# Splitting the 528-token stages at token 256 and giving weights and operands one address difference

## The chip, the core and the metric

The kernel runs on one core of one Trainium2 chip. The metric is the device time of one execution in microseconds (us), here the median of the runs shown; lower is better. One further execution is recorded by the hardware profiler, and all rows below come from that one.

## The reference

The reference runs two transformer-like blocks after one another on a sequence of 512 tokens with 1024 features, in float32. The first block has two layers, one with differential attention and one with chunked attention, each followed by a layer norm and a gated feed-forward of width 2816. The second block puts 16 learned "meta" tokens in front, so that it works on 528 tokens, and runs two layers of this form:

```
for l in range(DEPTH):
    h = h + hybrid_mixer(rmsnorm(h, norm_mix_g[l]), ...)     # gated linear attention, retention, LRU
    h = h + conv_glu_ffn(rmsnorm(h, norm_ffn_g[l]), ...)     # up, causal conv of 3, silu(gate)*val, down
return rmsnorm(h, final_norm_g)[:, N_META:]
```

Nearly all arithmetic is matrix products with weight matrices: 1024 x 3328 and 1024 x 1024 in a mixer, 1024 x 5632 (up) and 2816 x 1024 (down) in a feed-forward.

## The kernel before

**Numbers and tiles.** A float32 matrix product is made of three products in the format float32r. Each operand is split into a high part and a low part (XH and XL for the activations, WH and WL for the weights), and for each slice k of 128 inputs TensorE adds WL\*XH, WH\*XL and WH\*XH into PSUM. The helper `part` (line 756 of the profile, L756) issues these; the weight slice is the stationary operand (128 x 128), and the activations are the moving one. Every matmul loads its weights anew, so a LDWEIGHTS belongs to each of them; it overlaps the matmul before.

**Units.** The weights come in 534 units. A unit is one output tile of 128 columns with 8 slices of 128 inputs (1024 floats in a partition), or half of a 256-column tile, or one product of a down-projection (5 or 6 slices). SyncE's queue loads units from HBM into `raw`; ScalarE rounds them into WH (L1551, `highs`); VectorE subtracts to get WL (L2193, `lows`); WH and WL have three slots each, of W_PITCH = 1088 floats. `weight_places` says where in its slot a unit lies: "plain" puts slice k at 128\*k plus an offset; "turned" puts it at W_STEP\*((k + turn) % 4) + 128\*(k // 4), with W_STEP = 272. In the kernel before no unit is turned; the units that have an offset are those of the attention layers (48 floats) and the first three of b, f0 and f1 (16 floats).

**Stages.** In order: attention a, its output ao, feed-forward f0, attention b, output bo, feed-forward f1 (all 512 tokens), then mixer m0, its output mo0, feed-forward g0, mixer m1, output mo1, feed-forward g1 (528 tokens). Each feed-forward does 24 up tiles, the first down part (28 products, `down`, L1090), 20 up tiles, and the second down part (28 products). The down-projections are written with seven products of half-size operands in place of eight; their operands lie in FH and FL for f0 and f1, in GHH and GHL for g0 and g1: six slots with seven rows each. Sums of weight blocks that these products need are made by DMAs that GpSimd issues (`weight_sums`), and SyncE's queue fetches them.

**Segments.** 512 tokens fill one PSUM bank, so in the 512-token stages a tile has one moving segment of 512 columns. 528 tokens take two banks, and two segments. `tokens`, `two`, `pair_of` and `segments` put the split at token 272; the first segment ends its bank and the second starts the next one. In m0, mo0, g0 and m1 the segments are 272 and 256 columns; from mo1 on only the tokens from 14 are needed, and they are 258 and 256. The order in a tile is: for each k, for each of the three products, first segment, second segment:

```
for i, (wb, xb) in enumerate(((WL, xh), (WH, xl), (WH, xh))):
    for a, x0, x1 in segs:
        ins = nc.tensor.matmul(P[:, a:a + x1 - x0], weight(u, wb, k), xb[:, kx, x0 - c0:x1 - c0], ...)
```

`wide_tokens` (L854) makes the tiles of 256 output columns in the mixers: there the activations are stationary, a slice of 128 tokens that starts at token 16 + 128\*i, and the weights are moving, 256 columns. `hgrn` (L1354, L1356) and `ret_values` (L1448, L1453) multiply blocks of 128 tokens that start at token 16 and cut them at the split with `segments`.

**Memory plan.** What matters below is an operand's start in floats, modulo 64 (256 bytes), in a partition. XH, XL, WH and WL start at 32. The rows of XH and XL are 512 floats apart in the 512-token stages and 528 (16 modulo 64) in the others. GH and GL (what the mixers' outputs are multiplied from) start at 16 with rows of 528. FH and FL start at 16, rows of 256, slots of 1792 (0 modulo 64). GHH starts at 16 and GHL at 48, with rows of 272 and slots of 1904 (48 modulo 64); g1 uses 256 of each row. A weight slice in a plain unit starts at 32 plus the unit's offset, for every k.

## Time and profile before

| what | value |
|---|---|
| median of 3 runs | 2564.49 us (2563.74 to 2565.13) |
| the profiled execution, its own time | 2568.07 us |
| its span, first to last instruction | 2566.3 us |
| TensorE busy | 2520.3 us, 98% of the span |
| weight loads busy | 2296.5 us, 89% |
| VectorE busy | 1622.9 us, 63% |
| ScalarE busy | 1163.3 us, 45% |
| GpSimd busy | 169.4 us, 7% |
| matmul instructions in the record | 19246 |

A matmul's duration in the record runs from its start to the end of its last column, and neighbours overlap. So the pace of a stream is the distance from one start to the next, which a timeline gives over several matmuls and a window gives by its count. The profiled execution is 3.58 us longer than the median of the runs; its span is 1.8 us shorter than its own time.

### The profile page before, as it was taken

Reading aid. Unit: us, or ns where it says so; the run is one execution under the profiler, and the core shown is the slowest. Engines: PE = TensorE matmul, PEld = TensorE weight load, DVE = VectorE, ACT = ScalarE, POOL = GpSimd, SP = SyncE. Lnnn points to the kernel's source line nnn. Section 1 sums busy time; section 2 is a strip of 40 time slices with the busy share of each in tenths; the row PEclk is TensorE's granted clock in tenths of the full one; section 3 lists DMA queues with packets and bytes.
Section 4 is the critical chain, followed back from the end, with each engine's and each line's share of the span. In section 5 each row is a group of like instructions: output and inputs, shape, how many; then the busy total and the mean of one; then the engine's idle time right before and its main releaser. Section 6 shows DMA issues by size and latency. Waiting matters only on the chain.

```text
span 2566.3 us, 44717 instructions
## 1 busy us (share of the span) xinstructions
PE 2520.3 (98%) x19246; PEld 2296.5 (89%) x19246; DVE 1622.9 (63%) x2784; ACT 1163.3 (45%) x1924; POOL 169.4 (7%) x219
## 2 busy tenths in 40 slices
PE   9999999999999999999999999999999999999998
PEld 7777889889877888989899899999999989999998
DVE  5767756457566665546766557666675754766666
ACT  4554533335455443334554435434444534544443
POOL 0000200100000110110000011001000000200100
PEclk9999999999999999999999999999999999999999
DMA  5222955974322593895311249259652122954975
GB/s 192 89 66 70 255 150 162 294 193 147 103 82 65 158 248 97 268 256 164 140 67 51 69 160 259 84 174 287 157 187 93 65 71 97 263 143 141 291 175 163
DMA packets 104311, 397.33 MB, mean 155 GB/s; under 512 B 10416, under 2 KB 12720, under 8 KB 84272
## 3 DMA queue, kind: packets, MB, share of 16 engines
q1 hardware_dynamic: 60400, 249.07, 28.5%
q0 software_dynamic: 42992, 143.82, 23.9%
q8 instruction: 151, 2.47, 0.4%
q10 hardware_dynamic: 720, 1.57, 0.2%
q14 instruction: 48, 0.39, 0.0%
HBM read 383.80 MB, written 133.30 MB: 201 GB/s over the span
## 4 chain that ended last, share of the span: by engine, by line
PE 88%; DVE 6%; ACT 3%; DMA 2%; issue 1%; SPq 0%; POOL 0%; DVEq 0%; ACTq 0%; POOLq 0%
PE P L756 59%; PE P L1090 13%; PE P L854 3%; PE P L877 3%; PE P L763 2%; DVE WL L2193 2%; ACT WH L1551 1%; PE P L889 1%; DMA raw<-in_wts 1%; PE P L1188 1%; PE P L1209 1%; PE P L1302 1%; PE P L903 1%; PE P L935 1%; DVE X L2289 0%
## 5 line engine op out<-in xcount | busy, mean ns | idle before, releaser
L756 PE MATMUL P<-XH,WL 128*128 128x256 f32 (+3 forms) x3080 | 839.9, 322 | 15.1 <-DVE XL L2525 6.9
L756 PE MATMUL P<-XL,WH 128*128 128x256 f32 (+3 forms) x3080 | 817.0, 314 | 0.0
L756 PE MATMUL P<-XH,WH 128*128 128x256 f32 (+3 forms) x3080 | 816.7, 314 | 0.0
L2193 DVE TENSOR_TENSOR WL<-raw,WH 128x1024 fp32r<-128x1024 f32 (+2 forms) x533 | 573.9, 1079 | 317.7 <-ACT WH L1551 316.1
L1551 ACT ACTIVATE WH<-raw 128x1024 fp32r<-128x1024 f32 (+2 forms) x533 | 498.0, 941 | 465.9 <-PE P L756 223.4
L756 PEld LDWEIGHTS P<-XH,WL 128*128 128x128 f32 x3080 | 517.9, 189 | 61.2 <-DVE XL L2525 9.8
L756 PEld LDWEIGHTS P<-XH,WH 128*128 128x128 f32 x3080 | 516.3, 189 | 35.5
L756 PEld LDWEIGHTS P<-XL,WH 128*128 128x128 f32 x3080 | 515.8, 189 | 33.0
L1090 PE MATMUL P<-GHH,WL 128*128 128x272 f32 (+1 forms) x616 | 178.3, 290 | 9.5 <-DVE WL L2193 9.5
L1090 PE MATMUL P<-GHH,WH 128*128 128x272 f32 (+1 forms) x616 | 177.0, 287 | 0.0
L1090 PE MATMUL P<-GHL,WH 128*128 128x272 f32 (+1 forms) x616 | 177.0, 287 | 0.0
L1090 PE MATMUL P<-FH,WL 128*128 128x256 f32 x616 | 171.6, 279 | 1.9 <-DVE WL L2193 1.9
L1090 PE MATMUL P<-FH,WH 128*128 128x256 f32 x616 | 170.4, 277 | 0.0
L1090 PE MATMUL P<-FL,WH 128*128 128x256 f32 x616 | 170.4, 277 | 0.0
L3047 DVE SCALAR_TENSOR_TENSOR tmp<-P,PP,tmp 128x527 f32<-128x527 f32 (+1 forms) x88 | 66.7, 758 | 143.9 <-ACT tmp L2141 143.9
L689 POOL DMA_DIRECT2D sums<-in_quads x96 | 104.7, 1091 | 524.4 <-DMA sums<-in_quads 524.4
L1090 PEld LDWEIGHTS P<-GHH,WL 128*128 128x128 f32 x616 | 118.0, 192 | 10.9 <-DVE WL L2193 10.8
L2141 ACT ACTIVATE tmp<-P,PP 128x528 f32<-128x528 f32 (+1 forms) x88 | 68.7, 781 | 118.6 <-PE P L756 118.6
L1090 PEld LDWEIGHTS P<-FH,WL 128*128 128x128 f32 x616 | 115.6, 188 | 2.9 <-DVE WL L2193 2.7
L1090 PEld LDWEIGHTS P<-GHL,WH 128*128 128x128 f32 x616 | 118.2, 192 | 0.1
L1090 PEld LDWEIGHTS P<-GHH,WH 128*128 128x128 f32 x616 | 118.0, 192 | 0.0
L1090 PEld LDWEIGHTS P<-FH,WH 128*128 128x128 f32 x616 | 115.9, 188 | 0.0
(373 smaller groups left out, 3789.8 us busy)
## 6 DMA issues: line engine op xcount, KB each, us to landing
raw<-in_wts SPq DMA_DIRECT2D x151, 1024.0 KB, 5.0
sums<-in_quads POOLq DMA_DIRECT2D x32, 1152.0 KB, 28.5
sums<-in_quads POOLq DMA_DIRECT2D x32, 960.0 KB, 24.6
sums<-in_quads POOLq DMA_DIRECT2D x16, 1536.0 KB, 19.6
raw<-sums SPq DMA_DIRECT2D x64, 384.0 KB, 3.4
sums<-in_quads POOLq DMA_DIRECT2D x16, 1280.0 KB, 13.6
raw<-sums SPq DMA_DIRECT2D x64, 320.0 KB, 3.1
raw<-in_wts SPq DMA_DIRECT2D x48, 384.0 KB, 3.6
```

Of the source, the lines that this page charges most:

```text
L689: nc.gpsimd.dma_start(sums_dram[st, ph, mp, :, a:b, 0:n], term, accum_op=ALU.add).then_inc(summed[mp], 16)
L756: ins = nc.tensor.matmul(P[:, a:a + x1 - x0], weight(u, wb, k), xb[:, kx, x0 - c0:x1 - c0], start=start and i == 0, stop=stop and i == 2, ...
L763: ins = nc.tensor.matmul(P[:, a:a + x1 - x0], m, src[:, x0 - c0:x1 - c0], start=start, stop=stop)
L854: ins = nc.tensor.matmul(o, xb[:, k, c0:c1], weight(u + k // 4, wb, k % 4, 256), start=n == 0 and k == 0 and i == 0, stop=k == 7 and i == ...
L877: ins = nc.tensor.matmul(o, xb[:, k, c0 - c:c1 - c], weight(u + k // 4, wb, k % 4, 256), start=n == 0 and k == 0 and i == 0, stop=k == 7 a ...
L889: ins = nc.tensor.transpose(P[:, 512 * b + 128 * j:512 * b + 128 * j + 128], src[:, 128 * j:128 * j + 128], ident)
L903: nc.tensor.matmul(P[:, o:o + ke], q[64 * m:64 * m + 64, lane, 128 * i:128 * i + 128], k[64 * m:64 * m + 64, 2 + lane, 0:ke], start=(j == ...
L1090: ins = nc.tensor.matmul(P[:, 512 * b:512 * b + n], weight(u, wb, q), combined(st, xb, j, OPERAND[p]), start=p not in AFTER and q == 0 and ...
L1551: nc.scalar.activation(weight_rows(u, WH), raw_rows(u), ACT.Copy).then_inc(*act.up("whi", u))
L2141: nc.scalar.activation(y[:, a0:], pair_bank(n % 4)[:, a0:], ACT.Identity, bias=par("fcb", 44 * l + c), scale=PP[:, k:k + 1]).then_inc(*act ...
L2193: nc.vector.tensor_tensor(weight_rows(u, WL), raw_rows(u), weight_rows(u, WH).bitcast(F), ALU.subtract).then_inc(*dve.up("wlo", u))
L3047: nc.vector.scalar_tensor_tensor(y[:, a0 + 1:T], p[:, a0:T - 1], w(1), y[:, a0 + 1:T], ALU.mult, ALU.add).then_inc(*dve.up("conv1", l, n))
```

## The change

Nothing is computed differently except for the order of a few sums. Three things move:

1. The split lies at token 256 (MID): segments of 256 and 272 columns in m0, mo0, g0 and m1, and from mo1 on 256 and 258 (tokens 14 to 270 to 528). The PSUM places of a pair of banks move along.
2. The units of the mixers and of the up-projections of g0 and g1 are turned: slices 272 floats apart in four groups. ScalarE and VectorE write them as four rows of 256, and the host packs the blocks in that order. Turn is 0 for the 256-column units and the output tiles, 1 otherwise; mo1 and g1 also get 14 floats more. The products of the down-projections of g0 get an offset of 16 floats times the operand's row, those of g1 none.
3. GHH and GHL have slots of 1920 floats with rows of 272 in g0 and of 256 in g1.

```diff
@@ weight_places
-    place = [("plain", 0)] * len(plan)
+    place = [("plain", 0, 0)] * len(plan)
     def put(stage, n, kind, amount):
-        place[first[stage] + n] = (kind, amount)
+        place[first[stage] + n] = (kind, amount, 14 if stage in ("mo1", "g1") and kind == "turned" else 0)
...
+    for l in range(2):
+        for n in range(first[f"mo{l}"] - first[f"m{l}"]):
+            put(f"m{l}", n, "turned", 0 if plan[first[f"m{l}"] + n][4] == 256 else (1, 1)[l])
+        for n in range(8):
+            put(f"mo{l}", n, "turned", (0, 0)[l])
+        for ph, (m0, m1) in enumerate(UP_TILES):
+            at = first[f"g{l}B"] - 2 * (m1 - m0) - first[f"g{l}"] if ph else 0
+            for n in range(2 * (m1 - m0)):
+                put(f"g{l}", at + n, "turned", (1, 1)[l])
+            for n, (p, mp) in enumerate(products(ph)):
+                put(f"g{l}{'AB'[ph]}", n, "plain", LINE // 4 * ((OPERAND[p] + (-OPERAND[p] if l else 0)) % 4))
@@ segments of tokens
+MID = 256
 def two(p):
-    a = 1024 * p + 240
-    return [(a, 0, 272), (a + 272, 272, T)]
+    return [(1024 * p + 512 - MID, 0, MID), (1024 * p + 512, MID, T)]
 def segments(c0, c1):
-    return [(a, b) for a, b in ((c0, min(c1, 272)), (max(c0, 272), c1)) if a < b]
+    return [(a, b) for a, b in ((c0, min(c1, MID)), (max(c0, MID), c1)) if a < b]
+def mid(s):
+    return MID + META - 2 if s == 6 else MID
 def tokens(s):
-    return HV if s == 7 else [(META - 2 if s == 6 else 0, 272), (272, T)]
+    return HV if s == 7 else [(META - 2, mid(s)), (mid(s), T)] if s == 6 else [(0, mid(s)), (mid(s), T)]
@@ build
-        GHH = sb("GHH", [128, 6, 7, 272], R, ph)
-        GHL = sb("GHL", [128, 6, 7, 272], R, ph)
+        GHH = sb("GHH", [128, 6, 1920], R, ph)
+        GHL = sb("GHL", [128, 6, 1920], R, ph)
...
         def weight(u, f, k, n=128):
-            kind, at = place[u]
+            kind, turn, at = place[u]
             if kind == "plain":
-                a = at + n * k
+                a = turn + n * k
             elif n == 256:
-                a = W_STEP * ((k + at) % 4)
+                a = at + W_STEP * ((k + turn) % 4)
             else:
-                a = W_STEP * ((k + at) % 4) + 128 * (k // 4)
+                a = at + W_STEP * ((k + turn) % 4) + 128 * (k // 4)
...
         def combined(st, xb, j, i, n=1):
             w = 272 if st == 2 else 256
-            return xb[st][:, pair_slot(j), i, 0:w] if n == 1 else xb[st][:, pair_slot(j), i:i + n, 0:w]
+            rows = xb[st][:, pair_slot(j), :, :] if st < 2 else xb[st][:, pair_slot(j), 0:7 * w].rearrange("p (i t) -> p i t", t=w)
+            return rows[:, i, 0:w] if n == 1 else rows[:, i:i + n, 0:w]
...
@@ hgrn, ret_values
-                o = 1024 * 3 + 240
+                o = 1024 * 3 + 512 - MID
...
-                                         start=(a == 272), stop=False, skip_group_check=True)
+                                         start=(a == MID), stop=False, skip_group_check=True)
```

## Rows read from the trace of the kernel before

**Rows 1.** The page: busy time of each engine, and the chain that ended last.

```profile
PE 2520.3 (98%) x19246; PEld 2296.5 (89%) x19246; DVE 1622.9 (63%) x2784; ACT 1163.3 (45%) x1924; POOL 169.4 (7%) x219
...
PE 88%; DVE 6%; ACT 3%; DMA 2%; issue 1%; SPq 0%; POOL 0%; DVEq 0%; ACTq 0%; POOLq 0%
```

**Rows 2.** PE matmuls of L756 in windows: busy (x count), granted clock, DMA share, GB/s.

```profile
1730.00:1840.00 110.00, 110.00 (x906) 1.00 0.91 243
2385.00:2490.00 105.00, 105.00 (x883) 1.00 0.93 249
1070.00:1165.00 95.00, 95.00 (x421) 1.00 1.00 265
```

**Rows 3.** Timeline of PE in g0 up: start us, us; each row is one pair.

```profile
1777.88 0.40 PE L756 MATMUL P<-XH,WL 128*128 128x272 f32 x2
...
1778.36 0.41 PE L756 MATMUL P<-XH,WH 128*128 128x272 f32 x2
1778.61 0.41 PE L756 MATMUL P<-XH,WL 128*128 128x272 f32 x2
...
1780.80 0.40 PE L756 MATMUL P<-XH,WL 128*128 128x272 f32 x2
```

**Rows 4.** Timeline of PE in f1 down: start us, us.

```profile
1029.92 0.28 PE L1090 MATMUL P<-FH,WH 128*128 128x256 f32 x1
...
1030.94 0.28 PE L1090 MATMUL P<-FH,WH 128*128 128x256 f32 x1
```

**Rows 5.** Timeline of PE in f0 down: before and after a stall.

```profile
400.82 0.28 PE L1090 MATMUL P<-FH,WL 128*128 128x256 f32 x1
...
401.88 0.28 PE L1090 MATMUL P<-FH,WL 128*128 128x256 f32 x1
...
404.86 0.38 PE L1090 MATMUL P<-FH,WL 128*128 128x256 f32 x1 [0.34 <-DVE WL L2193]
405.08 0.28 PE L1090 MATMUL P<-FL,WH 128*128 128x256 f32 x1
...
406.57 0.28 PE L1090 MATMUL P<-FH,WH 128*128 128x256 f32 x1
```

**Rows 6.** PE by line and form: count, busy us, mean ns, idle before.

```profile
L756 PE MATMUL P<-XH,WL 128*128 128x272 f32 x672 | 206.6, 307 | 6.4 <-DVE XL L2525 3.3 <-DVE WL L2193 1.9 <-ACT tmp L2056 0.8
...
L756 PE MATMUL P<-XH,WL 128*128 128x258 f32 x352 | 100.1, 284 | 1.1 <-DVE XL L2525 0.9
...
L1090 PE MATMUL P<-GHH,WL 128*128 128x272 f32 x308 | 90.5, 294 | 4.6 <-DVE WL L2193 4.6
```

**Rows 7.** PE matmuls of L1090 in windows: g0 down, g1 down.

```profile
1860.00:1900.00 40.00, 40.00 (x322) 1.00 0.57 168
2335.00:2375.00 40.00, 40.00 (x341) 1.00 0.63 195
```

**Rows 8.** PE matmuls of L854 in one window of m1.

```profile
2075.46:2081.87 6.41, 6.41 (x54) 1.00 0.50 164
```

**Rows 9.** Timeline of PE in m0, the value products of one head.

```profile
1308.87 0.39 PE L1350 MATMUL P<-SD,VI 16*128 16x16 f32 x2
1309.19 0.49 PE L1354 MATMUL P<-SC,VI 128*128 128x128 f32 x2
```

**Rows 10.** VectorE writes of 768 floats: in one run, and as three rows.

```profile
L2377 DVE TENSOR_TENSOR FL<-SQ,FH 128x768 fp32r<-128x768 f32 x22 | 21.1, 959 | 6.8 <-ACT FH L1745 6.8
...
L2377 DVE TENSOR_TENSOR GHL<-GQ,GHH 128x768 fp32r<-128x768 f32 x11 | 10.6, 959 | 3.4 <-ACT GHH L1745 3.4
```

**Rows 11.** g0 up: busy PE, PEld, DVE, ACT, POOL; and a wait of VectorE.

```profile
1730.00:1840.00 110.00, 110.00 (x906) 110.00 (x906) 72.69 (x101) 49.17 (x66) 13.07 (x12) 1.00 0.91 243
...
DVE tmp L3047 <- ACT tmp L2141: 35.7, 15, 3.8
```

**Rows 12.** Timeline, g1: last sums DMA issued by POOL, first fetch on the SP queue.

```profile
2466.53 0.81 POOL L689 DMA_DIRECT2D sums<-in_quads  x1 [7.41 <-DMA sums<-in_quads]
...
2479.10 0.33 SPq L626 DMA_DIRECT2D raw<-sums  x1
```

More of the change, by code:

```diff
@@ L354, in pair_of @@
 def pair_of(p, s):
-    return [(1024 * p + 240 + a, a, b) for a, b in tokens(s)]
+    return [(1024 * p + 512 - mid(s) + a, a, b) for a, b in tokens(s)]
 HALF_BANK = {(6, 0): 3, (7, 0): 4, (6, 1): 5, (7, 1): 6}
@@ L517, in weight_rows @@
         def weight_rows(u, f, a=0, n=None):
-            kind, at = place[u]
+            kind, turn, at = place[u]
             if kind == "plain":
-                return f[:, u % NS, at + a:at + (length(u) if n is None else a + n)]
-            return f[:, u % NS, :].rearrange("p (j c) -> p j c", c=W_STEP)[:, :, 0:256]
+                return f[:, u % NS, turn + a:turn + (length(u) if n is None else a + n)]
+            g = f[:, u % NS, at:at + 3 * W_STEP + 256]
+            return bass.AP(g.tensor, g.offset, [list(g.ap[0]), [W_STEP, 4], [1, 256]])
         def raw_rows(u):
@@ L526, in weight @@
         def weight(u, f, k, n=128):
-            kind, at = place[u]
+            kind, turn, at = place[u]
             if kind == "plain":
-                a = at + n * k
+                a = turn + n * k
             elif n == 256:
-                a = W_STEP * ((k + at) % 4)
+                a = at + W_STEP * ((k + turn) % 4)
             else:
-                a = W_STEP * ((k + at) % 4) + 128 * (k // 4)
+                a = at + W_STEP * ((k + turn) % 4) + 128 * (k // 4)
             return f[:, u % NS, a:a + n]
@@ L581, in bank, with pair_bank @@
             return P[:, 512 * b:512 * b + n]
-        def pair_bank(p):
-            return P[:, 1024 * p + 240:1024 * p + 240 + T]
+        def pair_bank(p, s=4):
+            return P[:, 1024 * p + 512 - mid(s):1024 * p + 512 - mid(s) + T]
         def bank_a(g, n):
@@ L1432, in ret_values @@
                     yield
-                o = 1024 * 3 + 240
+                o = 1024 * 3 + 512 - MID
                 for n in range(2):
@@ L1448, in ret_values @@
                                 nc.tensor.matmul(P[s0:s0 + 64, o + a:o + b], VR[:, 1 + j, 64 * hh:64 * hh + 64],
-                                                 SCr[:, hh, a - META:b - META], start=(a == 272), stop=False, skip_group_check=True)
+                                                 SCr[:, hh, a - META:b - META], start=(a == MID), stop=False, skip_group_check=True)
                             for hf in range(2):
@@ L2140, in conv_glu @@
                         act.wait_ge(*at("cl", s, (m - 3) // 2, "t"))
-                    nc.scalar.activation(y[:, a0:], pair_bank(n % 4)[:, a0:], ACT.Identity, bias=par("fcb", 44 * l + c),
+                    nc.scalar.activation(y[:, a0:], pair_bank(n % 4, s - 1)[:, a0:], ACT.Identity, bias=par("fcb", 44 * l + c),
                                          scale=PP[:, k:k + 1]).then_inc(*act.up("tap", l, n))
@@ L2700, in residual @@
                     dve.wait_ge(x_back[m], 16 * (s // 2 - 1))
-                    nc.vector.tensor_tensor(X[:, m, a0:], X[:, m, a0:], pair_bank(m % 3)[:, a0:], ALU.add).then_inc(*dve.up("res", s, m))
+                    nc.vector.tensor_tensor(X[:, m, a0:], X[:, m, a0:], pair_bank(m % 3, s)[:, a0:], ALU.add).then_inc(*dve.up("res", s, m))
                     if m:
@@ L3035, in conv_glu @@
                     c = NF * j + m
-                    y, p = conv_buffer(m, j), pair_bank(n % 4)
+                    y, p = conv_buffer(m, j), pair_bank(n % 4, s - 1)
                     def w(i):
```

## The prediction

> **What bounds the kernel now.** I read the page first. TensorE is busy for 98% of the span and holds 88% of the chain that ended last [rows 1]. In such a kernel the busy share hides what matters: how far apart matmuls start. So I read paces next, from windows (a time by a count; a window also counts the one or two matmuls that overlap its edges) and from timelines (start to start).
>
> - f1 up, one segment of 512: 95 us by about 419, 226.7 ns, or 0.443 ns a column [rows 2].
> - f1 down, 256 columns: nine matmuls in 1.02 us, 113.3 ns, again 0.443 [rows 4].
> - g0 up, a pair of 272 and 256 columns: twelve pairs in 2.92 us, 243.3 ns, 0.461 a column [rows 3]. g1 up: 105 us by 881, 238.3 ns a pair of 514 columns, 0.464 [rows 2].
> - g0 down, 272 columns: 40 us by 320, 125.0 ns; g1 down, 256 columns: 40 us by 339, 118.0 ns; 0.460 and 0.461 [rows 7]. The 256-column tiles of the mixers: 118.7 ns, 0.464 [rows 8].
>
> The granted clock is 1.00 in all these windows, the 2.4 GHz level. So the same instruction on the same engine has two paces, 4% apart, and the whole second half of the program runs at the slow one.
>
> The memory plan says what differs. The overlap that counts is between a matmul and the weight load of the next. I call d the start of the moving operand less the start of the next weight slice, in floats modulo 64. In f0 and f1 down d is 16 - 32 = 48 at every matmul; in f1 up it is always 0. In g0 up the activations' rows step by 16 with k, the second segment adds 16 (272 is 256 + 16), and the weights step by 0: d goes through 0, 16, 32 and 48. In g0 down it changes with slot, row, and high or low part.
>
> One thing speaks against reading d as the whole cause: f0 down begins at the slow pace with the same d. Nine matmuls from 400.82 take 1.06 us, 117.8 ns or 0.460 a column; after the stall at 404.86 the stream settles at 113.3 [rows 5]. With d = 48 there are two steady paces, and what came before picks one. The slow one is, to 1%, the pace that g0 and g1 have now.
>
> **Part 1: the tiles of m, mo and g up.** After the change both segments start 16\*k past the base, since 256 is 0 modulo 64, and a turned slice lies at 16\*(k + turn). Turn 1 against XH (32 and 32), and turn 0 against GH (16 and 32), give d = 48 within a k; the 14 floats of mo1 and g1 cancel. "Order kept" leaves one exception: the last matmul of each k overlaps the load of slice k + 1, which lies 16 further, so d = 32 at one matmul in six.
>
> The columns do not change (272 + 256, 258 + 256). The counts are (672 + 64) \* 3 = 2208 pairs of 528 columns and (352 + 64) \* 3 = 1248 pairs of 514; rows 6 show 672 and 352 for one of the three products, and the 64 is eight output tiles by eight slices. At the fast pace a pair takes 233.7 and 227.5 ns: 9.6 and 10.8 ns less. The upper end is 21.2 + 13.5 = 34.7 us. The lower end is a stream that keeps the slow pace, 0.
>
> What does the step at each k cost? No row shows d = 32 inside a constant stream. The nearest row is how the stream finds back after a stall: 13 starts from 405.08 to 406.57 take 1.49 us against 1.47 at the fast pace, so 15 to 20 ns are lost before it runs fast [rows 5]. I charge 15 ns to every k, that is to three pairs. The 736 blocks of the first kind keep 28.8 - 15 = 13.8 ns (10.2 us), the 416 of the second 32.4 - 15 = 17.4 ns (7.2 us). **Gain 17.4 us**, half of the upper end.
>
> **Part 2: the down-projections of g0 and g1.** Slots of 1920 floats are 0 modulo 64, GHL then starts at 16 as GHH does, and the offset follows the row: d = 48 everywhere, with no step at k, as in f0 and f1. 308 \* 3 = 924 matmuls each, of 272 and of 256 columns [rows 6]. 125.0 to 120.4 ns and 118.0 to 113.3 ns: 4.3 + 4.3 = 8.6 us. In f0 three products of 28 ran slow before the stall [rows 5], and I expect the same entry: **gain 7.7 us**. Ends: 0 and 8.6.
>
> **Part 3: the 256-column tiles.** 192 \* 3 = 576 matmuls at 118.7 against 113.3 ns would be 3.1 us. They have the step at k too, so I take half, **1.5 us**.
>
> **Part 4: what the split adds.** `segments` cut nothing before, because the token blocks end at 144, 272 and 400. With the split at 256 the block 144 to 272 is cut, and a piece of 16 columns gets its own instruction: two for each of 8 heads in `hgrn`, eight in each layer's `ret_values`, 32 in all. The nearest row is another instruction of 16 columns with 128 outputs: its two passes start 0.32 us before what follows [rows 9], of which the columns need 0.03. Upper end 32 \* 0.29 = 9.3 us; lower end 0, where the neighbours cover it. Retention's pieces use half the array and run side by side, so I take half: **cost 4.6 us**.
>
> **What costs nothing, and its cover.** The 1024-float writes of turned units become four rows of 256. VectorE writes 768 floats in 959 ns both in one run (FL) and as three rows 272 apart (GHL in g1) [rows 10]. Even without that cover VectorE has room: in 110 us of g0 up it is busy for 72.7 and waits 35.7 us for ScalarE's reading of the tiles that TensorE delivers [rows 11]. It will wait less. Transfers keep their number, size and order on every queue. What is late next would be the sums of weight blocks. In g1 the last is issued at 2466.53 and first fetched at 2479.10 [rows 12], and up tiles shorter by 4 us do not close those 12.6 us.
>
> **The sum.** 17.4 + 7.7 + 1.5 - 4.6 = 22.0 us. The profiled execution took 2568.07 us (span 2566.3), so 2546.1; it lies 3.6 us above the median of the runs shown, which gives **2542.5 us**.
>
> **A rule against the change.** The rows show two paces for one shape, with the weight load beside each matmul the only other reader that the streams share [rows 3, 4]. The Trainium skill says otherwise (TensorE: Matmul & The Clock Gate, "Step-by-step: what each phase is for"): TensorE has "two independent SBUF read ports", and "Loading the next tile's weights doesn't steal SBUF read bandwidth from the running matmul." By that rule the address difference is nothing, and the sum would be part 4 alone. The trace doesn't agree that all streams of a shape run alike, but it can't say that addresses are the reason.
>
> **The rivals.**
> A. *The stream recovers within a k, at no cost.* For it: a constant stream at d = 48 stays fast for whole products [rows 4]. Against: the 15 to 20 ns after the stall. 34.7 + 8.6 + 3.1 - 4.6 = 41.8 us less: 2522.7.
> B. *The up tiles keep the slow pace.* For it: f0 down entered from continuous up tiles runs slow until it stalls [rows 5], and up tiles hardly stall: 6.4 us idle over 672 matmuls [rows 6]. Then only part 2 gains: 7.7 - 4.6 = 3.1, 2561.4.
> C. *Addresses do not matter; the pace belongs to having two segments, or to the engines beside.* For it: the rule above, and that the slow stages share 528 tokens. Against: g1 down has 256 columns and one segment, as f1 down has, and is slow [rows 4, 7]. +4.6: 2569.1.
> D. *Slower: with one difference the collision comes at every matmul instead of one in four.* Its place is the pairs of the up tiles. The price: pairs in g0 now start 0.24 or 0.25 us apart (1778.36 to 1778.61) [rows 3]; if all took 0.25, 6.7 ns more, 2208 would cost 14.8 us, and the 1248 others with the same 2.8% 8.2 us. With 7.7 back and 4.6 lost that is +19.9: 2584.4. It decides from 2.4 ns a pair on. Against: d = 48 is never slower than 0.460 in f0 and f1.
>
> **How the numbers follow.** Forecast 0.55, A 0.22, B 0.10, C 0.06, D 0.07. A measurement of this kernel can tell 0.2%, 5.1 us, from no change. Faster: the forecast, A, and a third of B, 0.80; same: the rest of B and C, 0.13; slower: D, 0.07. The range 2520 to 2562 holds the forecast with its bounds, A and B, and leaves out C and D.
>
> **What would show each step.** Right: timelines of g0 and g1 up show pairs near 239 and 233 ns, with a dearer one after each k; L1090 in g0 and g1 falls to 120.4 and 113.3 ns a start after its first stall; a window of VectorE there is busy for a larger share. A shows pairs of 233.7 throughout, B pairs of 243. Part 4 shows as 64 more TensorE records. Wrong would be: down-projections that stay at 125.0 and 118.0 ns (then d is not what decides), VectorE or the sums ending TensorE's idle time inside up tiles, or a granted clock below 1.00 in the windows of rows 2.

## The result and the profile after

The change makes the kernel 0.15% slower, less than the 0.2% that the prediction took for "no change", though the interval leaves out 1: median 2567.53 us (2564.53 to 2570.93, 20 runs) against 2563.93 us (2561.23 to 2568.49, 20 runs) of the kernel before, ratio 1.0015, 95% interval 1.0008 to 1.0021. The forecast was 2542.5 us, and its range ended at 2562. The profiled execution of the kernel after took 2566.83 us, its span is 2565.0 us.

Lines of the kernel after are 19 higher: `part` is L775, `down` L1109, the `lows` L2212. From its page, busy times:

```profile
PE 2516.3 (98%) x19310; PEld 2292.8 (89%) x19310; DVE 1622.9 (63%) x2784; ACT 1162.9 (45%) x1924; POOL 169.2 (7%) x219
```

[rows 1] had 2520.3 us and 19246 records. The 64 added records are part 4. TensorE is busy 4.0 us less, and the span is only 1.3 us shorter: idle time grew by 2.7.

The up tiles, PE matmuls of L775 in windows as long as those of [rows 2] (us, busy and count, granted clock, DMA share, GB/s), first g0, then g1:

```profile
1724.00:1834.00 110.00, 110.00 (x913) 1.00 0.93 251
2380.00:2485.00 105.00, 105.00 (x873) 1.00 0.94 253
```

In g0, 913 matmuls in 110 us in place of 906: 0.8% better. In g1, 873 in 105 us in place of 883: **1.1% worse**. By start distances over the whole part the mean is 120.95 ns against 121.79 in g0, and 120.7 against 119.3 in g1. The timeline of g0 up (start us, us; a row is a pair) shows pairs 0.24 us apart, as [rows 3] did, and no run of 0.234:

```profile
1778.00 0.40 PE L775 MATMUL P<-XH,WL 128*128 128x256 f32 x2
...
1778.48 0.41 PE L775 MATMUL P<-XH,WH 128*128 128x256 f32 x2
```

The down-projections, L1109 in the windows of [rows 7]:

```profile
1855.00:1895.00 40.00, 40.00 (x326) 1.00 0.57 171
2335.00:2375.00 40.00, 40.00 (x353) 1.00 0.61 195
```

326 in place of 322 in 40 us of g0 (the window begins 5 us earlier than in [rows 7], after the same stall), and 353 in place of 341 in g1. By start distances that is 123.6 against 125.3 ns in g0, and 113.5 against 118.2 in g1. So part 2 worked, fully so in g1. But TensorE now reaches the next up tiles before their weights. Around the first part's end in g1 TensorE waits for VectorE, and ScalarE, which VectorE waits for there, waits for the transfer of a unit (engine, line, what it waited for: us in total, times, longest):

```profile
PE P L775 <- DVE WL L2212: 2.0, 1, 2.0
```

```profile
ACT WH L1570 <- DMA raw<-in_wts: 4.3, 2, 3.9
```

The first line has no counterpart before; with 0.6 us in g0 it gives 2.6 us back. Most of it belongs to this one execution: the four other profiled kernels below that have the change's down-projections and ran this part at 113.3 ns without added waits in the up tiles show 0.4 or 0.5 us here and 0 to 0.3 in g0, and ScalarE's longest wait for a unit is 2.3 or 2.4 us there in place of 3.9. The same line in one of them (part 4 undone, below):

```profile
PE P L775 <- DVE WL L2212: 0.5, 1, 0.5
```

VectorE waits as much as before in g0 up (35.7 us in [rows 11]), since the tiles come at nearly the old pace:

```profile
DVE tmp L3066 <- ACT tmp L2160: 35.2, 15, 4.1
```

Part 4 is plain in the timeline of one head of `hgrn` in m0 (L1373 and L1375; pieces of 112 and 16 columns in turn):

```profile
1308.32 0.31 PE L1373 MATMUL P<-SC,VI 128*128 128x16 f32 x2
1308.47 0.38 PE L1375 MATMUL P<-hQ,S 128*128 128x16 f32 x2
1308.70 0.47 PE L1373 MATMUL P<-SC,VI 128*128 128x128 f32 x2
```

The four passes of 16 columns take 0.38 us, from 1308.32 to 1308.70. The value products of a head take 2.574 us in place of 2.127, those of a pair in `ret_values` 3.304 in place of 2.913: 8 \* 0.447 + 4 \* 0.391 = **5.1 us**.

**Why the two profiled spans stand in the other order than the medians.** After some stalls the granted clock is low for a stretch, in both kernels. A window of PE in g0's second down part, then the timeline there:

```profile
1847.00:1850.40 3.40, 3.40 (x16) 0.52 0.70 182
```

```profile
1846.84 0.60 PE L1109 MATMUL P<-GHH,WL 128*128 128x272 f32 x1 [2.55 <-DVE WL L2212]
1847.23 0.43 PE L1109 MATMUL P<-GHL,WH 128*128 128x272 f32 x1
...
1848.14 0.43 PE L1109 MATMUL P<-GHH,WH 128*128 128x272 f32 x1
```

After a wait of 2.55 us the clock is 0.52 for 3.4 us, the 1.2 GHz level, and starts are 0.227 us apart in place of 0.124: some 1.6 us lost. At corresponding places of the program it happens in one kernel's profile and not in the other's, both ways: the windows show six such stretches before and four after. That is 3 us in favour of after, and I see nothing in the change that would bring it.

### The profile page after: what moved, and what is told of

Same layout as the page of the kernel before. It is cut to its first block, busy times and chain, and to the rows that moved or that the text cites. A ratio compares the mean times of both kernels' runs of the same rounds, so it can differ in the third digit from the quotient of the medians.

```text
span 2565.0 us, 44845 instructions
## 1 busy us (share of the span) xinstructions
PE 2516.3 (98%) x19310; PEld 2292.8 (89%) x19310; DVE 1622.9 (63%) x2784; ACT 1162.9 (45%) x1924; POOL 169.2 (7%) x219
## 4 chain that ended last, share of the span: by engine, by line
PE 89%; DVE 6%; ACT 3%; DMA 2%; issue 1%; SPq 0%; POOL 0%; DVEq 0%; ACTq 0%; POOLq 0%
PE P L775 59%; PE P L1109 13%; PE P L896 4%; PE P L873 3%; PE P L782 2%; DVE WL L2212 2%; ACT WH L1570 1%; PE P L908 1%; DMA raw<-in_wts 1%; PE P L1207 1%; PE P L1228 1%; PE P L1321 1%; PE P L922 1%; PE P L954 1%; DVE X L2308 0%
## 5 line engine op out<-in xcount | busy, mean ns | idle before, releaser
L775 PE MATMUL P<-XH,WL 128*128 128x256 f32 (+3 forms) x3080 | 840.4, 322 | 17.9 <-DVE XL L2544 7.0
L775 PE MATMUL P<-XH,WH 128*128 128x256 f32 (+3 forms) x3080 | 817.6, 314 | 0.0
L775 PE MATMUL P<-XL,WH 128*128 128x256 f32 (+3 forms) x3080 | 815.0, 314 | 0.0
L2212 DVE TENSOR_TENSOR WL<-raw,WH 128x1024 fp32r<-128x1024 f32 (+2 forms) x533 | 573.8, 1079 | 318.6 <-ACT WH L1570 317.0
L775 PEld LDWEIGHTS P<-XH,WL 128*128 128x128 f32 x3080 | 523.1, 189 | 64.0 <-DVE XL L2544 9.6
L775 PEld LDWEIGHTS P<-XH,WH 128*128 128x128 f32 x3080 | 518.6, 188 | 35.7
L775 PEld LDWEIGHTS P<-XL,WH 128*128 128x128 f32 x3080 | 520.5, 189 | 33.1
L1109 PE MATMUL P<-GHH,WL 128*128 128x272 f32 (+1 forms) x616 | 176.8, 287 | 9.9 <-DVE WL L2212 9.9
L1109 PE MATMUL P<-GHH,WH 128*128 128x272 f32 (+1 forms) x616 | 175.4, 285 | 0.0
L1109 PE MATMUL P<-GHL,WH 128*128 128x272 f32 (+1 forms) x616 | 175.4, 285 | 0.0
L1109 PE MATMUL P<-FH,WL 128*128 128x256 f32 x616 | 171.6, 279 | 1.9 <-DVE WL L2212 1.9
L1109 PE MATMUL P<-FH,WH 128*128 128x256 f32 x616 | 170.4, 277 | 0.0
L1109 PE MATMUL P<-FL,WH 128*128 128x256 f32 x616 | 170.4, 277 | 0.0
L1109 PEld LDWEIGHTS P<-GHH,WL 128*128 128x128 f32 x616 | 118.0, 192 | 11.4 <-DVE WL L2212 11.3
L1109 PEld LDWEIGHTS P<-FH,WL 128*128 128x128 f32 x616 | 115.6, 188 | 2.9 <-DVE WL L2212 2.7
L1109 PEld LDWEIGHTS P<-GHL,WH 128*128 128x128 f32 x616 | 118.1, 192 | 0.1
L1109 PEld LDWEIGHTS P<-GHH,WH 128*128 128x128 f32 x616 | 118.0, 192 | 0.0
L1109 PEld LDWEIGHTS P<-FH,WH 128*128 128x128 f32 x616 | 115.9, 188 | 0.0
```

Of the source, the lines that this page charges most:

```text
L1109: ins = nc.tensor.matmul(P[:, 512 * b:512 * b + n], weight(u, wb, q), combined(st, xb, j, OPERAND[p]), start=p not in AFTER and q == 0 and ...
L2212: nc.vector.tensor_tensor(weight_rows(u, WL), raw_rows(u), weight_rows(u, WH).bitcast(F), ALU.subtract).then_inc(*dve.up("wlo", u))
```

## The experiments

All paces below are distances from one start to the next, or a window by its count (a window counts one or two matmuls more than fit in). Medians stand beside those of the kernel before on the same chip.

### Does the difference matter in a constant stream? (down-projections)

In f0 and f1, where the difference is 48 throughout, three of the four down parts get other offsets:

```diff
+    for stage, off in (("f0A", 16), ("f0B", 32), ("f1A", 48)):
+        for n in range(28):
+            put(stage, n, "plain", off)
```

> The kernel before with the weight slices of the down-projections of f0 and f1 moved by a constant: the difference d (moving operand less next weight slice, in floats modulo 64) is 32 in the first part of f0, 16 in its second part, 0 in the first part of f1 and stays 48 in the second part of f1. If the address difference decides the pace (theory 1), the parts run at different paces: 113.3 ns a matmul at 48 after the first stall, and something like 118 ns or more in at least two of the others, which costs about 2 us a part. If addresses do not matter (theory 2), all four parts run at 113.3 ns after their first stall.

Windows of 15 us at difference 32, 16, 0 and 48, PE matmuls of this kernel's `down`:

```profile
415.00:430.00 15.00, 15.00 (x129) 1.00 0.60 187
575.00:590.00 15.00, 15.00 (x130) 1.00 0.55 186
1025.00:1040.00 15.00, 15.00 (x127) 1.00 0.60 188
1190.00:1205.00 15.00, 15.00 (x135) 1.00 0.58 201
```

Means of 118.7, 117.8, 120.0 and 113.3 ns after the part's stall (one run, 2566.66 us, against 2565.42). The difference matters: the steady paces at 32 and at 0 are 118.7 and 120.0 ns, which 48 shows in no run, and among the four only 48 gives the fast pace. The addresses alone change 256 columns by up to 6%. For 16 this run alone isn't enough, since 117.8 is also the slow pace of 48; a run below adds stalls at 16, and it is at 117.8 after every one of them. Only the weights moved here. That it is the difference, and not the place of the weights, shows in two later runs, where the moving operand starts at 32 instead of 16: again 113.3 ns at 48, 117.8 at 16 and 120.0 at 0.

### The same for one segment of 512 columns

```diff
+    for l, ph, off in ((0, 0, ("plain", 16)), (0, 1, ("plain", 32)), (1, 0, ("plain", 48))):
+        m0, m1 = UP_TILES[ph]
...
+            put(f"f{l}", at + n, *off)
```

> The kernel before with the weight slices of the 512-column up tiles moved: d is 48 in the first part of f0, 32 in its second part, 16 in the first part of f1, 0 as before in the last. Theory 1 (address difference decides): 226.7 ns at 0 and more at others, up to 10 ns (4%) a matmul, so up to 5 us a part. Theory 2 (addresses do not matter): 226.7 ns in all four. A third possibility is that 512 columns leave enough room that only 256-column streams feel it: then also 226.7 in all.

Windows of 90 us at difference 48, 32, 16 and 0:

```profile
300.00:390.00 90.00, 90.00 (x388) 1.00 0.65 168
460.00:550.00 90.00, 90.00 (x389) 1.00 1.03 277
920.00:1010.00 90.00, 90.00 (x395) 1.00 0.64 168
1070.00:1160.00 90.00, 90.00 (x399) 1.00 1.05 286
```

By start distances 233.3, 232.4, 228.9 and 226.7 ns (one run, 2571.77 us, against 2565.42). For 512 columns the fast pace is at 0, where the kernel has it, and 48 is the worst of the four: it loses 6.6 ns. So 48 is no property of the operands by itself: the good difference goes with the number of columns.

### Two segments at one difference

The 512-column up tiles of f0 and f1 are cut in two; f0A and f1A have 256 + 256 at 48 throughout (one bank, two banks), f0B 272 + 256 at 48 (16 columns are summed twice, so the kernel's output is wrong and the run serves for its times alone), f1B turned units.

```diff
-                        tile(up_unit(U, n), one(b), hi, lo, c0=c)
+                        split_tile(up_unit(U, n), l, n, hi, lo, c)
...
+                for k in range(8):
+                    for i, (wb, xb) in enumerate(((WL, hi), (WH, lo), (WH, hi))):
+                        for j, (x0, x1) in enumerate(segs):
+                            ins = nc.tensor.matmul(P[:, o + x0:o + x1], weight(u, wb, k), xb[:, k, META - c + x0:META - c + x1], ...)
```

> The kernel before with the up tiles of f0 and f1 (tokens 0 to 512) written as two segments. First part of f0: 256 and 256 in one bank, d = 48 throughout, no step at a new k. Second part of f0: segments of 272 and 256 that both start at 0 modulo 64 and overlap in 16 columns (so 16 columns are summed twice), d = 48 throughout, one bank. First part of f1: 256 and 256 in two banks, d = 48. Second part of f1: 256 and 256 in one bank with turned weights, so that d goes through four values with k but is the same for both segments. Theory 1 (a constant difference gives the fast pace, and the step at each k is what the changed kernel lacks): 226.7 ns a pair in the first and third, 233.7 in the second, about 236 in the fourth. Theory 2 (having two segments in turn is what holds the slow pace): about 236 ns a pair in all with 256 and 256, 243 with 272 and 256. If only the change of bank matters, the third is slow and the first is not. The one bank or two makes no other difference to what is computed.

Windows of 100 us in f0A and f0B:

```profile
300.00:400.00 100.00, 100.00 (x852) 1.00 0.61 158
455.00:555.00 100.00, 100.00 (x836) 1.00 1.00 269
```

All four stay slow: by start distances 235.6, 240.0, 235.6 and 236.1 ns a pair, and 240.0 for 272 + 256 is barely under the 241.7 of the kernel after with its step at every k. This looked like rival C, "the pace belongs to having two segments". The down-projections of the same run spoke against so simple a cause: all had d = 48; f0A and f1A both reached 113.3 ns within some six matmuls of the slow up tiles, with no stall between, and f1A's own stall then moved it to 117.8.

### The down-projections alone

```diff
-        GHH = sb("GHH", [128, 6, 7, 272], R, ph)
+        GHH = sb("GHH", [128, 6, 1920], R, ph)
...
+                put(f"g{l}{'AB'[ph]}", n, "plain", LINE // 4 * ((OPERAND[p] + (-OPERAND[p] if l else 0)) % 4))
```

> The kernel before with part 2 of the change alone: slots of 1920 floats and the offsets of the down products of g0 and g1, split at 272 as before. From the changed kernel's trace (123.3 ns a matmul in g0, 113.3 in g1 after the first stalls, against 125.0 and 118.0): theory 1 says 924 * 1.7 + 900 * 4.7 ns = 5.8 us less than the kernel before, if nothing else moves. Theory 2 (addresses do not matter, the paces of the changed kernel came from elsewhere): no difference.

2562.50 us (11 runs) against 2565.42, ratio 0.9988, interval 0.9979 to 0.9997: a gain of 2.9 us. In windows of 25 us its g0 down has 205 matmuls and its g1 down 223, the same as the kernel after. So part 2 was a gain, and the rest of the change lost it and 3.6 us more.

### Stalls in the two-segment stream

The up tiles of f0 and f1 are cut in two as under "Two segments at one difference", now 256 + 256 at 48 in all four parts, and TensorE waits before every fourth tile for the reading of the tile before it (not in f1B); f0B and f1B finish one segment before the other.

```diff
+                if n % 4 == 0 and (l, n >= 24) != (1, True):
+                    pe.wait_ge(*at("mul", l, n // 2 - 1))
```

> Kernel before with the 512-column up tiles of f0 and f1 cut into two segments of 256 columns at difference 48 throughout. Parts: f0A turns the two segments matmul by matmul, as the kernel does, in one bank; f1A the same in two banks; f0B finishes the first segment (24 matmuls) before the second; in these three TensorE waits before every fourth tile for the reading of the tile before it. f1B finishes one segment before the other and has no added waits. Theory 'history' (two steady paces, a stall draws which one follows; up tiles kept the slow one because they hardly stall): after some of the added stalls all four arms run at 113.3 ns per 256 columns, the turned ones too; of some six stalls an arm at least two are followed by it. Theory 'turns' (a stream that changes between two segments at one weight slice cannot take the fast pace): f0A and f1A stay at 117.8 ns after every stall; f0B and f1B reach 113.3 in part. Theory 'k step within a unit of eight slices' (fast only in the downs for another reason): all four stay at 117.8.

Timeline of f0A around the second added stall (start us, us; a row is a pair):

```profile
308.14 0.40 PE L869 MATMUL P<-XH,WL 128*128 128x256 f32 x2
...
309.08 0.40 PE L869 MATMUL P<-XL,WH 128*128 128x256 f32 x2
```

```profile
314.82 0.47 PE L869 MATMUL P<-XH,WL 128*128 128x256 f32 x2 [0.87 <-DVE tmp L2575]
...
315.83 0.39 PE L869 MATMUL P<-XL,WH 128*128 128x256 f32 x2
...
316.28 0.39 PE L869 MATMUL P<-XH,WL 128*128 128x256 f32 x2
```

Before the stall four pairs take 0.94 us, 235 ns each. At 314.82 there is a wait of 0.87 us; from 315.83 to 316.28 two pairs take 0.45 us. Windows of 10 us before and after that stall, in f1A and in f1B:

```profile
297.50:307.50 10.00, 10.00 (x87) 1.00 1.08 261
320.50:330.50 10.00, 10.00 (x91) 1.00 1.09 256
...
978.00:988.00 10.00, 10.00 (x90) 1.00 0.30 107
1100.00:1110.00 10.00, 10.00 (x91) 1.00 1.02 410
```

87 becomes 91 (90 or 91 by where the edges fall), 113.3 ns, and it stays so to the end of the part, but for the tile after each later stall (115.3). All of f0B and f1B runs at 113.3, and so does f1A, which was there before its first added stall. The first stall of f0A, at 291 us, had changed nothing. So **the pace is a state of the stream**: matmuls in turn between two segments can run at 113.3, and what they ran at two runs before was the state in which they happened to begin. "Turns" is out, and with it rival C.

A stall is not the only thing that moves the state. Where f0A's up tiles end, at 113.3 ns, the first down part begins at 117.8 with no idle time between (nine starts in 1.06 us), though d is 48 on both sides:

```profile
405.34 0.28 PE L1122 MATMUL P<-FH,WL 128*128 128x256 f32 x1
...
406.40 0.28 PE L1122 MATMUL P<-FH,WL 128*128 128x256 f32 x1
```

And the same stall does not always lead to the same pace. The first down part of f1 has the same instructions in the kernel after and in the run "A constant difference in g0 and g1" below, and in both one wait of 0.34 us at 1017 us. Windows of 15 us behind it, L1109 of the kernel after, then L1127 of the other:

```profile
1025.00:1040.00 15.00, 15.00 (x135) 1.00 0.59 193
```

```profile
1025.00:1040.00 15.00, 15.00 (x130) 1.00 0.58 187
```

113.3 ns in one, 117.8 in the other. Over all profiled executions of this document, 74 down parts have 256 columns at difference 48, and 17 of them ran at 117.8 behind the stall near their start (in g1 alone 5 parts out of 17). Each such part costs some 1.8 us. What decides it is not shown.

### Constant differences of 16, 0 and 32 in g down

```diff
-                put(f"g{l}{'AB'[ph]}", n, "plain", LINE // 4 * ((OPERAND[p] + (-OPERAND[p] if l else 0)) % 4))
+                put(f"g{l}{'AB'[ph]}", n, "plain", LINE // 4 * ((... + {(0, 0): 2, (0, 1): 3, (1, 0): 1, (1, 1): 0}[l, ph]) % 4))
```

> Kernel before with the change's part for the down-projections, but other constant differences: g0A 16, g0B 0 (272 columns), g1A 32, g1B 48 (256 columns). If the difference decides as it did with 256 columns in f0 and f1 (117.8, 120.0, 119, 113.3 ns): g1A 119, g1B 113.3, and the 272-column parts scale to 125.2 at 16 and 127.5 at 0. If 272 columns (17 groups of 16) run the moving operand through all differences anyway: g0A and g0B both stay at 123.3 as at 48. If only the constancy counts: all at 123.3 and 113.3.

Windows of g0A (difference 16), g0B (0), g1A (32) and g1B (48):

```profile
1700.00:1720.00 20.00, 20.00 (x160) 1.00 0.58 167
1880.00:1900.00 20.00, 20.00 (x162) 1.00 0.56 160
2357.00:2372.00 15.00, 15.00 (x128) 1.00 0.59 167
2528.00:2548.00 20.00, 20.00 (x179) 1.00 0.58 172
```

272 columns take 126.6 ns at 16 and 125.3 at 0, against 123.6 at 48; 256 columns 118.7 at 32 and 113.4 at 48, as in f0 and f1. The difference moves 272 columns as well, by less, and 48 is the best of the three (32 was not tried). But its 0.454 ns a column is never the 0.443 that I had taken for it.

### Stalls in the kernel after, and other widths

```diff
+                        if n % 4 == 0 and n < 24:
+                            pe.wait_ge(*at("tap", l, n - 1))
                         tile(up_unit(U, n), pair_of(p, 4 + 2 * l), XH, XL)
```

> Kernel after, with added waits: in the up tiles before token 24 of the count (part A) of g0 and g1, TensorE waits before every fourth tile until ScalarE has read the tile before it; part B has none. Also the 512-column tiles of f0 and f1 are cut in two, in turn, with a wait before every fourth tile: f0A 272 + 256 columns at difference 48 (16 columns of the second are summed twice), f0B 258 + 256 at 48 (2 columns twice), f1A 256 + 256 at 16, f1B 256 + 256 at 0. Theory 'history, and the step at k undoes it': g0A and g1A stay at 241 to 242 ns a pair after every wait, or fall to the fast pace for one k and return; f0B and f0A reach the fast pace after a wait if 258 and 272 columns allow it at all: 227.5 and 233.7 ns a pair. Theory 'history alone': g0A and g1A reach 233.7 and 227.5 ns a pair after one of the waits and g0B, g1B keep it. Theory 'only whole multiples of 64 columns': f0A and f0B stay at 240.2 and about 240 ns. f1A 235.6 ns throughout and f1B 240, if the difference 48 is needed, 226.7 if the waits alone decide.

Windows of 10 us between stalls: 272 + 256 at 48, 258 + 256 at 48 (both sum some columns twice, so this run too serves for its times alone), 256 + 256 at 16 and at 0, then the change's own tiles in g0 and g1:

```profile
318.00:328.00 10.00, 10.00 (x86) 1.00 1.09 243
515.00:525.00 10.00, 10.00 (x86) 1.00 1.08 230
990.00:1000.00 10.00, 10.00 (x87) 1.00 0.29 107
1133.50:1143.50 10.00, 10.00 (x85) 1.00 1.08 257
1637.50:1647.50 10.00, 10.00 (x85) 1.00 1.10 227
2306.00:2316.00 10.00, 10.00 (x86) 1.00 1.09 228
```

No arm reaches 91. The tiles after every stall are at 240.0, 240.0, 235.6 and 240.0 ns a pair, and the change's own at 241.7 in g0. So of what was tried, stalls help only at difference 48 with 256 + 256; the segments that the kernel has, 272 + 256 and 258 + 256, are not fast at this one constant difference. Other constant differences were not tried for these pairs.

### A constant difference in g0 and g1, without and with stalls

Base is the kernel after without the cut blocks and with plain units in the second layer (below). Rows of the activations are 576 floats apart, the eighth in a buffer of its own; so d is 48 at the change of k too.

```diff
+        self.x = x[:, :, :].rearrange("p k t -> p (k t)")[:, 0:4032].rearrange("p (k t) -> p k t", t=576)
...
+                put(f"g{l}", at + n, "plain", 16 + 14 * l)
```

> The kernel of e7 with a truly constant difference in g0 and g1 up: rows of the activations 576 floats apart (a multiple of 64; the eighth row in a buffer of its own) and plain units, so that d is 48 at every matmul, the change of k too. Segments stay 256 + 272 and 256 + 258, no added waits. Theory 'the step at k is what kept the slow pace, and natural stalls at the start of a stage suffice': g1 up falls from 238.6 to 227.5 ns a pair, 11 us less than e7 over 1056 pairs, and g0 up as much if 272 columns can be fast (another 8 us): ratio 0.991 to 0.995. Theory 'entry at the slow pace is kept': 240.2 ns a pair in g0 (1.5 ns * 1056 = 1.6 us less than e7), about 237 in g1: ratio 0.997 to 0.998.

```profile
1725.00:1835.00 110.00, 110.00 (x919) 1.00 0.93 252
2375.00:2480.00 105.00, 105.00 (x865) 1.00 0.95 258
```

2558.33 us (11 runs) against 2563.80, ratio 0.9982 (0.9973 to 0.9990). g0 has 919 matmuls in 110 us, 120.0 ns, in place of the change's 913; g1 only 865 in 105 us, **121.7 ns**, worse than the 119.3 of the kernel before, whose difference runs through all values. What g0 gains g1 loses: against its base, which has the ratio 0.9985 (0.9976 to 0.9994, below), this run can't be told apart.

> As e10, with TensorE waiting for ScalarE's reading of the tile before it at tiles 4, 8, 12, 28 and 32 of g0 and g1 up: ten stalls of some 1 us each, 10 us in all. Theory 'history': from one of them on, pairs run at 227.5 ns in g1 (up to 11 us back) and, if 272 columns allow it, 233.7 in g0 (7 us): against e10 between 7 us faster and, if both were fast already, 10 us slower. Theory 'these widths are never fast': 10 us slower than e10.

2581.97 us (5 runs) against 2563.80, ratio 1.0073 (1.0059 to 1.0087): some 24 us above the run without stalls, more than twice the 10 us that I had priced the stalls at. One reason is in the trace: the first added stall of g0 takes 4.1 us and the first of g1 4.0, and starts 0.22 us apart follow each. The tiles between the stalls keep 120.0 and 121.7 ns. No stall brings these widths to the fast pace.

### What does the step at k do where the widths can be fast?

As the cut tiles of f0 and f1 above, a wait before every fourth tile; f0A 320 + 192, f0B 288 + 256, f1A 384 + 128 columns at 48, and f1B 256 + 256 with the change's pattern. It reads shifted columns for this, so its output is wrong and only its times count.

```diff
+SEGS = {(0, False): ((0, 320), (320, 512)), (0, True): ((0, 288), (256, 512)), (1, False): ((0, 384), (384, 512)), (1, True): ((0, 256), (256, 512))}
...
+    for l, ph, off in ((0, 0, ("plain", 16)), (0, 1, ("plain", 16)), (1, 0, ("plain", 16)), (1, 1, ("turned", 1))):
...
+                            ins = nc.tensor.matmul(P[:, o + x0:o + x1], weight(u, wb, k), xb[:, k, slice(x0 - j * 64 + 16 * (k % 4), x1 - j * 64 + 16 * (k % 4)) if (l, n >= 24) == (1, True) else slice(META - c + x0, META - c + x1)],
```

> Kernel before with the 512-column tiles of f0 and f1 cut in two, in turn, a wait before every fourth tile. f0A 320 + 192 columns, f0B 288 + 256 (32 columns summed twice), f1A 384 + 128, all at difference 48; f1B 256 + 256 with the change's pattern: 48 within a k and 32 at its last matmul (the columns read are shifted by 16 per k, so its sums are of other tokens). Theory 'the matmuls must be whole multiples of 64 columns': f0A and f1A reach 0.443 ns a column, 226.7 ns a pair, after a wait; f0B stays near 0.46 (250 ns a pair of 544, fast would be 240.9). Theory 'multiples of 32': f0B fast too. Theory 'only 256': none of the three. f1B: if the step at k undoes the fast pace, pairs near 235.6 with a dearer one after each k, 706 to 725 ns per k; if only widths mattered in the change, 680 to 695 ns per k (my forecast's 15 ns a k gives 695).

Windows of 10 us between stalls:

```profile
299.00:309.00 10.00, 10.00 (x80) 1.00 1.08 261
476.00:486.00 10.00, 10.00 (x83) 1.00 1.00 409
983.00:993.00 10.00, 10.00 (x73) 1.00 0.59 159
1190.00:1200.00 10.00, 10.00 (x87) 1.00 1.07 261
```

f1B has 87, the slow count. By start distances the six matmuls of a k take 708 ns after three of its waits and 702 on the mean (696 and 708 in turn) after the two others, where six at the fast pace take 680 and six at the slow one 707. So the step at k alone undoes the fast pace. The three other widths miss too, and none of my three theories on widths had foreseen how: 320 + 192 takes 257.8 ns, 384 + 128 takes 285, and 288 + 256 takes 250.0 or 246.7 depending on the stall before, where 256 + 256 takes 226.7 or 235.6. With 384 + 128 the next start comes 226 ns after the long one and 59 after the short one: the short segment is brief, but the long one takes far more than the 170 ns of its columns at the fast pace. Why is not shown.

### Part 4 undone, and the second layer's units plain

```diff
-    return [(a, b) for a, b in ((c0, min(c1, MID)), (max(c0, MID), c1)) if a < b]
+    return [(a, b) for a, b in ((c0, min(c1, 272)), (max(c0, 272), c1)) if a < b]
```

> Kernel after, but hgrn and ret_values keep their cut at token 272 and their old place in the pair of banks, so the 32 added pieces of 16 columns are gone and everything else of the change stays. My forecast's part 4 was 4.6 us: expected about 2563 (ratio to before 0.9995). If the pieces are hidden by their neighbours: no change against the kernel after, 2567 to 2568 (ratio 1.0015). If each costs its upper end: 9.3 us less, 2558. The two traces of m0 and m1 differ by the same: half of it in each.

2563.52 us (11 runs) against 2564.96, ratio 0.9992 (0.9984 to 1.0001), where the kernel after had 1.0015: 4.0 us less by the medians, 5.9 by the ratios. The value products of a head are back at 2.13 us. The traces' 5.1 us and my 4.6 are both inside what this can tell.

Then the same with plain units in m1, mo1 and g1 up:

```diff
-    for l in range(2):
+    for l in range(1):
         for n in range(first[f"mo{l}"] - first[f"m{l}"]):
```

> The kernel of the run before with the units of m1, mo1 and g1 up plain again (their split stays at token 256, or 270 in g1); down-projections keep the change. Theory 'the turned units of the second layer cost time' (g1 up at 120.7 ns a matmul against 119.3, m1 some 2 us more): about 2 * 1.4 + 2 = 5 us less than the run before, ratio to before about 0.998. Theory 'the split in the other order costs it, not the addresses': within 1 us of the run before.

2560.42 us (11 runs), ratio 0.9985 (0.9976 to 0.9994). Its g1 up:

```profile
2378.00:2483.00 105.00, 105.00 (x873) 1.00 0.96 258
```

873 in 105 us, as in the kernel after. So what slowed g1 up was not the turned units, as I had it, but **the new split**: 256 columns from token 14 and 258 from 270, in place of 258 and 256 from 272. Whether by the order of the widths or by where the second segment starts wasn't tried apart. The 3.1 us between the two medians I can't place; the two intervals overlap.

### The parts that gained

Kernel before, with the change's down-projections, and for g0 up alone the split at 256 and rows 576 apart.

```diff
-    return HV if s == 7 else [(META - 2 if s == 6 else 0, 272), (272, T)]
+    return HV if s == 7 else [(0, 256), (256, T)] if s == 4 else [(META - 2 if s == 6 else 0, 272), (272, T)]
...
+            put("g0", at + n, "plain", 16)
```

> Kernel before with the change's down-projections, and for g0 up alone the split at token 256 with rows 576 floats apart (d = 48 at every matmul). Mixers, mo1 and g1 up stay as before, no block is cut. From e4: 2.9 us gained; from e10: g0 up at 120.1 against 121.8 ns over 2094 matmuls, 3.6 us. If parts add up: 6.5 us less than before, ratio 0.9975, and faster than e10 (0.9982). If g0's gain is not real: 0.9988 as e4.

Windows of its g0 and g1 up:

```profile
1722.00:1832.00 110.00, 110.00 (x919) 1.00 0.93 252
2372.00:2477.00 105.00, 105.00 (x884) 1.00 0.96 260
```

2556.03 us (6 runs) against 2563.69, ratio 0.9968, interval 0.9956 to 0.9980. It beats both kernels: 7.7 us under the kernel before by the medians. In its profiled execution (2557.86 us) neither g1 down part took the fast pace: 215 matmuls in 25 us, 117.8 ns, where the kernel after had 223. An execution that draws the fast pace in both should be up to 4 us shorter, (117.8 - 113.5) \* 924; that is an estimate. TensorE's wait for the up tiles between the two g1 parts is 0.2 us here.

## Why the prediction was wrong

**What bounds the kernel** was read rightly. TensorE stays at 98%, the clock is 1.00 in the windows, the two paces exist, and what decides between them is the address difference together with what came before: at a fixed shape one constant alone moves 256 columns from 113.3 to 120.0 ns. [rows 5] had shown the second half of this, and I used it only as the price of an entry.

**Part 1 is the step that failed.** It expected 17.4 us from 3456 pairs. It took two things for granted that no row showed:

- That 272 + 256 and 258 + 256 columns have the fast pace, 0.443 ns a column, because 256 columns and 512 have it. They don't: at a constant 48, after stalls or not, 272 + 256 take 240.0 ns a pair, and 258 + 256 take 240.0 from token 0 and 243.3 in g1's own order from token 14. In g0 that leaves 3.4 ns a pair (243.4 - 240.0) of the 9.6 that I charged as the upper end, in g1 a loss of 5. 272 columns alone are at 123.6 ns at 48 and slower at 16 and 0.
- That the stream recovers after the step at every k, for 15 ns. Where the widths do allow it the step holds the stream near the slow pace: 702 to 708 ns a k in place of my 695. My price came from a stall, after which nothing disturbs the stream; here the next step comes six matmuls later.

What came instead: g0 up gained 0.85 ns \* 2112 = 1.8 us, and g1 up lost 1.4 \* 2112 = 3.0 us, by its new split. I had given that move no cost. The tiles of the mixers gained about 2 us.

**Part 2** was forecast at 7.7 us. By paces it brought (125.3 - 123.6) \* 924 + (118.2 - 113.5) \* 924 = 5.9 us: all of it in g1, and 1.6 in place of 4.3 in g0, since 272 columns are at 123.6 and not at 120.4. Then 2.6 us went into waits for weights at the ends of the parts, which I had not named. I had looked for what is late next among the sums and found 12.6 us of room; the unit that was late is an ordinary one, the first up tile's behind the down part. In the profiled execution of the kernel after, its transfer was late as well; the four others show 0.5 to 0.7 us in all. Alone part 2 gained 2.9 us by the medians. The gain in g1 is partly chance: 5 of 17 such parts in the traces ran at 117.8 ns.

**Part 3** was 1.5 us; the tiles of 256 output columns went from 117.6 to 117.4 ns, 0.2 us. **Part 4** was 4.6 us and cost 5.1. **What costs nothing** held for VectorE's four-row writes: it waits for ScalarE as before.

Together: -1.8 + 3.0 - 2 - 5.9 + 2.6 - 0.2 + 5.1 = +0.8 us. The medians say +3.6 (2.1 to 5.4 by the ratio), the profiled spans -1.3, or about +2 without the two stretches at the low clock. So for the two profiled executions some 1 us stays unplaced. For the medians the waits are better put at 0.5 to 0.7 than at 2.6, and the sum at about -1: then some 3 to 6 us stay unplaced, of which the slow draws of g1's down parts would explain about 1 (an estimate: 5 of 17 parts at 1.8 us, two parts an execution).

**The rivals.** B was nearest, with 2561.4: up tiles that keep the slow pace, for the reason that they hardly stall. Its outcome holds, its reason is half of it: added stalls do nothing here, because of the widths and the step. Of C, the addresses do matter, against the sentence of the Trainium skill that I quoted (TensorE: Matmul & The Clock Gate, "Step-by-step: what each phase is for"): by that rule the place of the next weights is nothing, and the runs don't agree, since 256 columns take 113.3 ns at one difference and 120.0 at another, with the weights alone moved. D, dearer pairs in all up tiles, did not come as a whole; in g1 the pairs did get 2.8 ns dearer, but with plain units and the new split they are as dear, so its mechanism isn't what did it. A, the full fast pace, falls with the widths and the step. No rival priced the new split in g1; with it, and with part 2 at the 2.9 us that it gained alone, B ends above the kernel before.

## What to carry to other kernels

Before a pace is moved from one shape to another, try the shape: a fast pace of 256 and of 512 columns says nothing of 272 + 256, and 256 columns were best at a difference of 48 and 512 at 0. Where a stream has two steady paces, look at what it did last: a constant stream keeps what it has for hundreds of matmuls, a stall or the change to another stream may move it either way, and a short periodic disturbance holds it at the slow one. One trace is then one draw: 17 of 74 parts took the slow pace here, so a gain of 2 us in one profile needs the medians beside it. And test a change of layout by parts, since here the down-projections gained 3 us and g0 up 2, while the cut blocks and g1 up lost 8.

## What was not expected of the hardware

- A stall of 0.87 us moved a stream of 256-column matmuls at one constant difference from 117.8 to 113.3 ns for the rest of its part, some 800 matmuls; the same stall one time earlier did not. Behind the same wait of 0.34 us in the same part of the program, two executions ran at 113.3 and at 117.8 ns.
- The pace of two streams at one difference changed where one followed the other without idle time, from 113.3 to 117.8 ns in one run and from 117.8 to 113.3 in another.
- Two segments of unequal width cost up to 50 ns a pair more than two equal ones of the same sum: 285 ns for 384 + 128, 257.8 for 320 + 192, 235.6 at the slow pace of 256 + 256.
- 258 columns and 256 in turn are faster when the difference runs through all values (119.3 ns) than at a constant 48 (121.7 from token 14, and 120.0 from token 0 in the cut tiles).
- After a wait of 2.55 us the granted clock was at its 1.2 GHz level for 3.4 us. It does not follow each such wait.
